# The attention gates of the second block: token columns as stationary operand, 48 weight columns moving

## The chip, the cores and the metric

The kernel runs on one core of one Trainium2 chip. The metric is the device time of one execution in microseconds (us), the median of several. The engines named below are TensorE (PE for its matmuls, PEld for the loads of its stationary operand, which overlap the matmuls), VectorE (DVE), ScalarE (ACT), GpSimd (POOL) and the queue that starts the DMAs (SP).

## The reference

Two transformer blocks over 256 tokens of width 2048, in float32. The change is in the second block, where each of 8 heads has three gates per token (24 columns), which weigh its three attentions:

```
h = modulate(rms_norm_2(x, pre_norm_mix), shift_m, scale_m)      # 256 x 2048
(q_n, k_c, v_c, k_s, v_s, k_w, v_w, g_n, q_m, k_m, v_m) = jnp.split(h @ w_in, split_at, axis=-1)
gates = jax.nn.sigmoid(g_n)                                      # 256 tokens x 24
o_n = g[..., 0:1] * o_c + g[..., 1:2] * o_s + g[..., 2:3] * o_w  # per head
```

So the gate logits are the product of h (256 x 2048) with 24 columns of w_in.

## The kernel before, in words

Every large product is made from values split in two parts, a high one of reduced precision (whi, hH) and the rest (wlo, hL), as three products: high by high, low by high, high by low. A weight unit is a tile of 128 x 1024 (two slices of 128 rows by 512 columns). SP loads it into one of four buffers `raw`; ScalarE writes whi from it (`hi`, L562), VectorE writes wlo (`lo`, L1626), and TensorE makes 12 matmuls of 128x512 from it (`group`, all recorded on L1155, the line of the helper `mm`). Activations are stationary there (128 x 128), weights move.

h of the second block lies transposed in hH and hL: 128 partitions by 16 slices (KT) of 2048 rows, by 256 tokens. The 24 gate columns are loaded once, and split into wgh (ScalarE, L945) and wgl (VectorE, L2116), some 60 us before they are used. The order of the work is written out by hand for each engine. The gates belong to the fourth group of the projections: after unit u of that group TensorE runs a unit of the compression (`cmp_unit`, 16 matmuls with a stationary operand of 60 columns and 128 moving), and after that of unit 0 `gates_mm` (L1497): 48 matmuls, with 24 weight columns stationary and all 256 tokens moving, whose result is 24 x 256. After unit 3 ScalarE applies the sigmoid to it (L982); after unit 5 TensorE turns it back by two transposes (`gates_turn`, L1511), and after unit 7 ScalarE copies the turned 128 x 48 into `gates` (L986), which the attentions read from about 1614 us on. The units of VectorE's loop in this group are L2164 and after, two `lo` for each u.

The engines run ahead of each other only so far as buffers allow: whi and wlo have NSPLIT buffers, and the semaphore w_used tells when TensorE has finished with one.

Of the kernel before, what the change touches and what calls it, by code (L numbers as in the profile page):

```python
# [20 lines left out]
F32 = mybir.dt.float32  # L21
F32R = mybir.dt.float32r
U8 = mybir.dt.uint8
ACT = mybir.ActivationFunctionType
ALU = mybir.AluOpType
AX = mybir.AxisListType
ds = bass.ds

P = 128
T = 256  # L30
TT = T // P
D = 2048
KT = D // P
H = 8
DA = H * P
N_GATE = 24
# [19 lines left out]
BLK = H * T  # L56
# [121 lines left out]
def build(nc, A, out, scratch):  # L178
    with ExitStack() as ctx:
        def sb(name, shape, dt=F32):  # L180
            return ctx.enter_context(nc.sbuf_tensor(name, shape, dt))
# [3 lines left out]
        def S(name):  # L185
            if name not in sems:
                sems[name] = ctx.enter_context(nc.semaphore(name))
            return sems[name]
# [5 lines left out]
        hH = sb("hH", [P, KT, T], F32R)  # L194
        hL = sb("hL", [P, KT, T], F32R)
        yH = sb("yH", [P, H, T], F32R)
        yL = sb("yL", [P, H, T], F32R)
        arena = sb("arena", [P, 11 * BLK + BLK // 2])
# [13 lines left out]
        modA = sb("modA", [P, 4, KT])  # L212
        stat = sb("stat", [P, 4, 3, 2])
        gates = sb("gates", [P, TT, N_GATE])
        wgh = sb("wgh", [P, KT, N_GATE], F32R)
        wgl = sb("wgl", [P, KT, N_GATE], F32R)

        acc = ctx.enter_context(nc.psum_tensor("acc", [P, 2, 2 * GCOL], F32))
        W = ctx.enter_context(nc.psum_tensor("W", [P, 4, 512], F32))
# [8 lines left out]
        def C(name, n=P):  # L228
            return cst[:, CONST[name]:CONST[name] + n]
# [4 lines left out]
        ident, ones = C("ident"), C("ones")  # L234
# [58 lines left out]
        swung = [tokens(b[:, 1024:2048]) for b in turns]  # L293
        wg = blk(7)[:, 0:KT * N_GATE].rearrange("p (k n) -> p k n", k=KT)
        w2 = blk(7)[:, 384:384 + 2 * P].rearrange("p (k n) -> p k n", k=2)
        gateT = arena[0:N_GATE, 11 * BLK + 768:11 * BLK + 768 + T]
        ext = arena[0:H, 10 * BLK:10 * BLK + EXT]
        brow = [blk(0)[:, 1024 + n * GCOL:1024 + (n + 1) * GCOL] if n < 2 else blk(2)[:, n % 2 * GCOL:(n % 2 + 1) * GCOL]
                for n in range(8)]
# [15 lines left out]
        for h in range(H):  # L315
            hd, g = slice(h * T, (h + 1) * T), h // 4
# [236 lines left out]
        def _(act):  # L553
# [68 lines left out]
            for u in range(8):  # L622
                act.wait_ge(S(f"x_in{u}"), 16)
                for j in (2 * u, 2 * u + 1):
                    ins = act.activation(hH[:, j], x0[:, j], ACT.Identity, scale=V("norm_mix", 1, j))
# [316 lines left out]
            root(2)  # L942
            modulated(2, 0, 0, acc[:, (PHASES["cmp_kv"][1] + 1) % 2])
            act.wait_ge(S("wg_in"), 48)
            act.activation(wgh[:], wg[:], ACT.Copy).then_inc(S("wg_hi"), 1)  # L945

            def values(g, v, dst):

# [12 lines left out]
            v2, gg = PHASES["cmp_kv"][0], PHASES["cmp_kv"][1]  # L961
# [16 lines left out]
                act.activation(hsg, hidS, ACT.Sigmoid).then_inc(S("hid_sig"), 1)  # L978

            def gates_sig():  # L980
                act.wait_ge(S("gates_mm"), 1)
                act.activation(gateT, W[0:N_GATE, 2, 0:T], ACT.Sigmoid).then_inc(S("gates_sig"), 1)  # L982

            def gates_copy():
                act.wait_ge(S("gates_turn"), 1)
                act.activation(gates[:].rearrange("p t n -> p (t n)"), W[:, 2, 0:TT * N_GATE], ACT.Copy)\  # L986
                   .then_inc(S("gates_in"), 1)

            def kvc_copy():
                act.wait_ge(S("cmp_kv"), 1)  # L990
# [3 lines left out]
            for u in range(8):  # L994
                hi()
                hi()
                if u == 4:
                    headed(2, gg + 2, qn[:, 1024:2048])()
                if u == 3:
                    gates_sig()  # L1000
                if u == 7:
                    gates_copy()
            pl.g += 1
            group(hooks={3: values(gg + 3, v2 + 39, vsel), 4: hid_sig, 6: headed(3, gg + 3, arena[:, 1024:1536], GCOL),
                         7: kvc_copy})
# [2 lines left out]
            n = N_B  # L1008
# [24 lines left out]
            n = N_N  # L1033
# [117 lines left out]
        def _(pe):  # L1151
            pl = Place()

            def mm(o, l, r, start, stop):
                return pe.matmul(o, l, r, start=start, stop=stop, skip_group_check=True)  # L1155
# [308 lines left out]
            def rope_turn(e, g, heads=GT):  # L1464

                def run():
                    pe.wait_ge(S("roped"), e + 1)
                    for m in range(heads):
                        for t in range(TT):
                            ins = pe.transpose(acc[:, g % 2, m * T + t * P:m * T + (t + 1) * P],  # L1470
                                               roped[e][:, t, m * P:(m + 1) * P], ident)
                    ins.then_inc(S("rope_turn"), 1)
                return run
            gg = PHASES["cmp_kv"][1]
# [22 lines left out]
            def gates_mm():  # L1497

                pe.wait_ge(S("wg_lo"), 1)
                for k in range(KT):  # L1500
                    o = W[0:N_GATE, 2, 0:T]
                    mm(o, wgh[:, k], hH[:, k], k == 0, False)
                    mm(o, wgh[:, k], hL[:, k], False, False)
                    ins = mm(o, wgl[:, k], hH[:, k], False, k == KT - 1)
                ins.then_inc(S("gates_mm"), 1)

            def gates_turn():

                pe.wait_ge(S("gates_sig"), 1)
                for t in range(TT):  # L1510
                    ins = pe.transpose(W[:, 2, t * N_GATE:(t + 1) * N_GATE], gateT[:, t * P:(t + 1) * P],  # L1511
                                       ident[0:N_GATE, 0:N_GATE])
                ins.then_inc(S("gates_turn"), 1)

            def hidden_turn():

# [6 lines left out]
            def compressed():  # L1523
# [3 lines left out]
                for g in range(2):  # L1527
                    ins = mm(W[:, 0, T + g * P:T + (g + 1) * P], hid[:, 1, g], w2[:, 1], True, True)
                ins.then_inc(S("cmp_kv"), 1)
            also_sel = {0: gates_mm, 2: rope_turn(2, gg + 2), 5: gates_turn}  # L1530
            hooks = {u: also(cmp_unit(u // 4, u % 4), also_sel.get(u, lambda: None)) for u in range(8)}
            group(8, hH, hL, (("headed", 2),), hooks=hooks)
            group(8, hH, hL, (("headed", 3),), hooks={1: hidden_turn, 2: rope_turn(3, gg + 3, 2), 5: compressed})
# [2 lines left out]
            n = N_B  # L1536
# [20 lines left out]
            n = N_N  # L1557
# [53 lines left out]
        def _(dve):  # L1611
# [48 lines left out]
            def group(units=8, hooks={}, begin=0):  # L1660
                for u in range(begin, units):
                    lo()
                    if u in hooks:
                        hooks[u]()
                pl.g += 1
# [447 lines left out]
            dve.wait_ge(S("row_cols"), 1)  # L2113
            modulated(2, 2, 0, 0, acc[:, (PHASES["cmp_kv"][1] + 1) % 2])
            dve.wait_ge(S("wg_hi"), 1)
            dve.tensor_tensor(wgl[:], wg, wgh[:].bitcast(F32), ALU.subtract).then_inc(S("wg_lo"), 1)  # L2116

            def rotated(e, g, v, heads=GT):

                def run():
                    dve.wait_ge(S("w_used"), v)
                    if e in (0, 3, 4):
                        dve.wait_ge(S("kv_in"), (0, 3, 4).index(e) + 1)
                    if e:
                        dve.wait_ge(S("rope_turn"), e)
                    h = lambda x: x[:, :, 0:heads * P].rearrange("p t (h d) -> p t h d", d=P)
                    if e == 0:
                        dve.wait_ge(S("rope_in"), 16)
                    tab = lambda name: tokens(rope[name]).unsqueeze(2).to_broadcast([P, TT, heads, P])  # L2130
                    a, r, w = h(tokens(acc[:, g % 2])), h(roped[e]), h(swung[e])
                    d = P // 2
                    dve.tensor_tensor(r, a, tab("cos"), ALU.mult)
                    dve.tensor_tensor(w[..., 0:d], a[..., d:P], tab("sin")[..., 0:d], ALU.mult)
                    then(dve.tensor_tensor(w[..., d:P], a[..., 0:d], tab("sin")[..., d:P], ALU.mult))
                    dve.tensor_tensor(r, r, w, ALU.add).then_inc(S("roped"), 1)
                return run

            def blocks(kind):

                def run():
                    dve.wait_ge(S("headed"), 1)
                    base = arena[:, 0:1]
                    src = bass.AP(base.tensor, base.offset + kind * 2 * T,
                                  [list(base.ap[0]), [1, CMP_LEN], [T, 2], [CMP_STRIDE, N_CMP]])
                    pos = V("v_pos" if kind else "k_pos", CMP_LEN)
                    pos = bass.AP(pos.tensor, pos.offset, [list(pos.ap[0]), [1, CMP_LEN], [0, 2], [0, N_CMP]])
                    o = cx[:, kind * 1024:kind * 1024 + 960].rearrange("p (l g c) -> p l g c", g=2, c=N_CMP)
                    dve.tensor_tensor(o, src, pos, ALU.add).then_inc(S("cx"), 1)
                return run  # L2150

            def blocks_low(kind):
                def run():
                    src = cx[:, kind * 1024:kind * 1024 + 960].rearrange("p (l c) -> p l c", c=30)
                    dve.wait_ge(S("cx_hi"), kind + 1)
                    dve.tensor_tensor(cxp[kind][:, :, 1], src, cxp[kind][:, :, 0].bitcast(F32), ALU.subtract)\
                       .then_inc(S("cx_lo"), 1)
                return run
# [15 lines left out]
            v2, gg = PHASES["cmp_kv"]  # L2174
            group(begin=6)
            pl.phase("qn")
            group(hooks={3: rotated(0, gg, v2 + 8, 2)})
            group(hooks={1: blocks(0), 2: blocks(1), 3: rotated(1, gg + 1, v2 + 16), 6: blocks_low(0), 7: blocks_low(1)})
            for u in range(8):
                lo(2)  # L2180
                if u == 1:
                    rotated(2, gg + 2, v2 + 24)()
            pl.g += 1
            group(hooks={3: also(hidden_rows, rotated(3, gg + 3, v2 + 39, 2)), 5: hidden})
            pl.phase("moba")
            n = N_B
# [15 lines left out]
            n = N_N  # L2202
# [167 lines left out]
```

## Time and profile before

| | |
|---|---|
| median of 3 runs | 2623.61 us (2621.7 to 2624.24) |
| time of the profiled execution | 2621.29 us |
| its span | 2619.5 us |
| mean granted TensorE clock | 0.998 of full |
| PE busy | 2589.9 us (99% of the span) |
| DVE, ACT, POOL busy | 1745.3, 1232.0, 16.5 us |

The span is that of the profiled execution from its first to its last instruction; the time has some 1.8 us around it. PE at 99% does not say that every matmul runs at its peak: a busy TensorE may be waiting inside for its own load of the stationary operand.

### The profile page before, as it was taken

What the parts mean: (1) busy time and instruction counts of PE and PEld (TensorE: products, weight loads), DVE (VectorE), ACT (ScalarE), POOL (GpSimd) and SP (SyncE); (2) the same over time, 40 slices, a digit from 0 to 9 for tenths busy, and PEclk for the clock granted to TensorE, in tenths of its full rate; (3) what the DMA queues carried; (4) which work ended last, traced back from release to release, by engine and by line L of the source; (5) the groups of instructions that cost most, each with busy time, mean ns of one, the idle gap of its engine ahead of it and who ended that gap; (6) DMA issues with size and microseconds to landing.
All of it is one profiled execution on the core that took longest, in us unless ns stands there. A gap on an engine that the chain in (4) does not pass through costs nothing.

```text
span 2619.5 us, 34483 instructions
## 1 busy us (share of the span) xinstructions
PE 2589.9 (99%) x12128; PEld 2158.3 (82%) x12128; DVE 1745.3 (67%) x2106; ACT 1232.0 (47%) x1476; POOL 16.5 (1%) x24
## 2 busy tenths in 40 slices
PE   9999999999999999999999999999999999999998
PEld 7888888888888888888888788888778888888886
DVE  6777668666457777777777777875665555555565
ACT  6444456554454444444444545555544444444343
POOL 0000000000000000000000000000000000000000
PEclk9999999999999999999999999999999999999999
DMA  8876667676558888888877677774466666766664
GB/s 302 279 234 207 214 200 237 200 233 220 191 185 258 256 256 255 251 252 253 253 252 254 182 238 232 218 223 144 139 215 218 210 214 198 230 210 214 210 212 141
DMA packets 281096, 582.27 MB, mean 222 GB/s; under 512 B 17904, under 2 KB 28288, under 8 KB 280336
## 3 DMA queue, kind: packets, MB, share of 16 engines
q1 hardware_dynamic: 279376, 574.25, 69.4%
q0 software_dynamic: 1600, 6.38, 0.8%
q8 instruction: 81, 1.33, 0.2%
q14 instruction: 39, 0.32, 0.0%
HBM read 578.44 MB, written 2.11 MB: 222 GB/s over the span
## 4 chain that ended last, share of the span: by engine, by line
PE 92%; DVE 3%; DMA 2%; ACT 1%; issue 1%; SPq 0%; DVEq 0%; ACTq 0%
PE acc L1155 86%; PE W L1155 4%; DMA raw<-in_w_in 2%; PE W L1204 1%; DVE wlo L1626 1%; DMA raw<-in_w_ada_t 1%; ACT whi L562 1%; PE W L1332 0%; DVE arena L2251 0%; DVE raw L1639 0%; PE acc L1470 0%; PE W L1300 0%; DVE arena L1802 0%; ACT arena L591 0%; ACT arena L634 0%
## 5 line engine op out<-in xcount | busy, mean ns | idle before, releaser
L1626 DVE TENSOR_TENSOR wlo<-raw,whi 128x1024 fp32r<-128x1024 f32 x888 | 1080.6, 1224 | 756.3 <-ACT whi L562 754.2
L562 ACT ACTIVATE whi<-raw 128x1024 fp32r<-128x1024 f32 x888 | 934.1, 1059 | 1123.8 <-PE acc L1155 968.5
L1155 PE MATMUL acc<-whi,hH 128*128 128x512 f32 x2528 | 688.3, 394 | 6.4 <-ACT whi L562 4.0
L1155 PE MATMUL acc<-wlo,hH 128*128 128x512 f32 x2528 | 676.5, 389 | 1.7 <-DVE wlo L1626 1.7
L1155 PE MATMUL acc<-whi,hL 128*128 128x512 f32 x2528 | 676.8, 389 | 0.1
L1155 PEld LDWEIGHTS acc<-wlo,hH 128*128 128x128 f32 x2528 | 474.4, 188 | 102.0 <-DVE wlo L1626 2.6
L1155 PEld LDWEIGHTS acc<-whi,hL 128*128 128x128 f32 x2528 | 474.4, 188 | 101.0 <-DVE hL L1681 1.0
L1155 PEld LDWEIGHTS acc<-whi,hH 128*128 128x128 f32 x2528 | 468.2, 188 | 101.9 <-issue 8.6
L1155 PE MATMUL acc<-whi,yH 128*128 128x512 f32 x992 | 269.5, 393 | 0.0
L1155 PE MATMUL acc<-wlo,yH 128*128 128x512 f32 x992 | 265.4, 389 | 0.0
L1155 PE MATMUL acc<-whi,yL 128*128 128x512 f32 x992 | 265.3, 389 | 0.0
L1639 DVE CUSTOM_DVE_ANT_0 raw<-raw,crow 128x1024 f32<-128x1024 f32 x192 | 234.1, 1219 | 8.6 <-DMA raw<-in_w_ada_t 8.6
L1155 PEld LDWEIGHTS acc<-whi,yL 128*128 128x128 f32 x992 | 186.2, 188 | 39.1
L1155 PEld LDWEIGHTS acc<-wlo,yH 128*128 128x128 f32 x992 | 186.2, 188 | 39.0
L1155 PEld LDWEIGHTS acc<-whi,yH 128*128 128x128 f32 x992 | 185.0, 188 | 37.1
L1155 PE MATMUL W<-arena 128*128 128x128 f32 (+2 forms) x650 | 104.2, 301 | 4.5 <-POOL arena L517 2.6
L1155 PEld LDWEIGHTS W<-arena 128*128 128x128 f32 x650 | 90.2, 194 | 11.8 <-POOL arena L517 2.6
L805 ACT ACTIVATE arena<-arena,stat 128x128 f32<-128x128 f32 x80 | 34.9, 437 | 51.5 <-DVE stat L1948 51.4
L2044 DVE TENSOR_TENSOR arena<-arena,acc 128x1024 f32<-128x1024 f32 x44 | 53.5, 1216 | 0.3 <-PE acc L1155 0.3
L2272 DVE TENSOR_TENSOR yL<-W,yH 128x1024 fp32r<-128x1024 f32 x14 | 17.1, 1224 | 49.6 <-ACT yH L1084 49.6
L1084 ACT ACTIVATE yH<-W 128x1024 fp32r<-128x1024 f32 x14 | 14.4, 1026 | 71.8 <-PE W L1204 71.8
L1204 PE MATMUL W<-cst,arena 128*128 128x128 f32 x312 | 41.0, 275 | 4.8 <-DVE arena L1687 4.8
(192 smaller groups left out, 944.2 us busy)
## 6 DMA issues: line engine op xcount, KB each, us to landing
raw<-in_w_in SPq DMA_DIRECT2D x264, 512.0 KB, 4.7
raw<-in_w_ada_t SPq DMA_DIRECT2D x192, 512.0 KB, 4.8
raw<-in_w_ffn_in SPq DMA_DIRECT2D x176, 512.0 KB, 4.5
raw<-in_w_up SPq DMA_DIRECT2D x128, 512.0 KB, 4.4
raw<-in_w_down SPq DMA_DIRECT2D x128, 512.0 KB, 4.4
raw<-in_w_ffn_out SPq DMA_DIRECT2D x88, 512.0 KB, 4.9
raw<-in_w_out SPq DMA_DIRECT2D x32, 512.0 KB, 4.4
raw<-in_w_o SPq DMA_DIRECT2D x32, 512.0 KB, 3.8
```

The lines of the kernel that those rows point to most:

```text
L562: act.activation(whi[:, v], raw[:, s], ACT.Copy).then_inc(S("w_hi"), 1)
L805: ins = act.activation(p, p, ACT.Exp, bias=stat[:, 1, n % 3, t:t + 1], scale=1.0 if kind == "bias" else SCALE, accum_out=stat[:, 2, n % 3, ...
L1084: act.activation(dst[:, 4 * h:4 * h + 4], tiles(turned), ACT.Copy).then_inc(S("f2_hi"), 1)
L1155: return pe.matmul(o, l, r, start=start, stop=stop, skip_group_check=True)
L1204: ins = pe.transpose(ps[:, m * T + t * P:m * T + (t + 1) * P], src[:, t, m * P:(m + 1) * P], ident)
L1626: dve.tensor_tensor(wlo[:, v], raw[:, s], whi[:, v].bitcast(F32), ALU.subtract)\
L1639: dve.tensor_tensor_reduce(raw[:, s], raw[:, s], crow[:, pl.j % 2 * UW:(pl.j % 2 + 1) * UW], 1.0, 0.0, ALU.mult, ALU.add, o).then_inc(S("u ...
L2044: dve.tensor_tensor(x, x, tokens(acc[:, (PHASES["ffn1"][1] + g) % 2]), ALU.add).then_inc(S("ff_sum"), 1)
L2272: dve.tensor_tensor(lo[:, q], tiles(turned), hi[:, q].bitcast(F32), ALU.subtract).then_inc(S("f2_lo"), 1)
```

## The change

The roles of the operands are exchanged. wgh and wgl become the halves of one tile wgp of 16 x 48 columns. For each of the two token tiles, TensorE loads 128 columns of hH as stationary operand and moves all 48 columns of wgp, then loads the same 128 columns of hL and moves the 24 of wgh. The result has tokens on partitions, in two halves of 24 columns for each token tile (the second half holds high by low). A `tensor_reduce` of VectorE adds the halves into `gates`, and the sigmoid works in place there. The two transposes and the copy are gone.

```
-        wgh = sb("wgh", [P, KT, N_GATE], F32R)
-        wgl = sb("wgl", [P, KT, N_GATE], F32R)
+        wgp = sb("wgp", [P, KT, 2 * N_GATE], F32R)
+        wgh, wgl = wgp[:, :, 0:N_GATE], wgp[:, :, N_GATE:]
...
             def gates_sig():
-                act.wait_ge(S("gates_mm"), 1)
-                act.activation(gateT, W[0:N_GATE, 2, 0:T], ACT.Sigmoid).then_inc(S("gates_sig"), 1)
-
-            def gates_copy():
-                act.wait_ge(S("gates_turn"), 1)
-                act.activation(gates[:].rearrange("p t n -> p (t n)"), W[:, 2, 0:TT * N_GATE], ACT.Copy)\
-                   .then_inc(S("gates_in"), 1)
+                act.wait_ge(S("gates_sum"), 1)
+                g = gates[:].rearrange("p t n -> p (t n)")
+                act.activation(g, g, ACT.Sigmoid).then_inc(S("gates_in"), 1)
...
                 pe.wait_ge(S("wg_lo"), 1)
-                for k in range(KT):
-                    o = W[0:N_GATE, 2, 0:T]
-                    mm(o, wgh[:, k], hH[:, k], k == 0, False)
-                    mm(o, wgh[:, k], hL[:, k], False, False)
-                    ins = mm(o, wgl[:, k], hH[:, k], False, k == KT - 1)
+                for t in range(TT):
+                    o = W[:, 2, t * 2 * N_GATE:(t + 1) * 2 * N_GATE]
+                    for k in range(KT):
+                        c = slice(t * P, (t + 1) * P)
+                        mm(o, hH[:, k, c], wgp[:, k], k == 0, False)
+                        ins = mm(o[:, 0:N_GATE], hL[:, k, c], wgh[:, k], False, k == KT - 1)
                 ins.then_inc(S("gates_mm"), 1)
-
-            def gates_turn():
-
-                pe.wait_ge(S("gates_sig"), 1)
-                for t in range(TT):
-                    ins = pe.transpose(W[:, 2, t * N_GATE:(t + 1) * N_GATE], gateT[:, t * P:(t + 1) * P],
-                                       ident[0:N_GATE, 0:N_GATE])
-                ins.then_inc(S("gates_turn"), 1)
...
-            also_sel = {0: gates_mm, 2: rope_turn(2, gg + 2), 5: gates_turn}
+            also_sel = {0: gates_mm, 2: rope_turn(2, gg + 2)}
...
+            def gates_sum():
+
+                dve.wait_ge(S("gates_mm"), 1)
+                parts_of = W[:, 2, 0:TT * 2 * N_GATE].rearrange("p (t h n) -> p t n h", t=TT, h=2)
+                dve.tensor_reduce(gates[:], parts_of, AX.X, ALU.add).then_inc(S("gates_sum"), 1)
             for u in range(8):
                 lo(2)
                 if u == 1:
                     rotated(2, gg + 2, v2 + 24)()
+                if u == 2:
+                    gates_sum()
```

On TensorE, behind the compression unit of u = 0, the order before has 48 gate matmuls, which go through these three kinds 16 times; further down, behind the compression unit of u = 5, stand the two transposes (the shape is that of the result: 24x256 is a stationary operand of 24 columns with 256 moving):

```order
L1155 MATMUL W<-wlo,yH 60x128
L1155 MATMUL W<-hH,wgh 24x256
L1155 MATMUL W<-hL,wgh 24x256
L1155 MATMUL W<-hH,wgl 24x256
...
L1155 MATMUL acc<-whi,hH 128x512 x4
...
L1511 MATMUL W<-cst,arena 128x24 x2
```

With the change there are 64 at the same place, in 32 pairs of these two kinds (128x48 is a stationary operand of 128 columns with 48 moving), and the row of L1511 is gone:

```order
L1148 MATMUL W<-wlo,yH 60x128
L1148 MATMUL W<-wgp,hH 128x48
L1148 MATMUL W<-wgp,hL 128x24
...
L1148 MATMUL acc<-whi,hH 128x512 x4
L1148 MATMUL acc<-whi,hL 128x512 x4
```

So 48 pairs of a narrow load and a wide matmul become 64 pairs of a wide load and a narrow matmul, in the place where they stood.

On VectorE, in the same group, the order before, from the rope arithmetic of u = 1 (L2133 to L2136) on:

```order
L2133 TENSOR_TENSOR arena<-acc,arena 128x1024 [waits rope_turn,w_used]
L2134 TENSOR_TENSOR arena<-acc,arena 128x8x64
L2135 TENSOR_TENSOR arena<-acc,arena 128x8x64
L2136 TENSOR_TENSOR arena<-arena 128x1024 [waits dve_step]
L1626 TENSOR_TENSOR wlo<-raw,whi 128x1024 [waits w_hi] x16
L2163 COPY arena<-W 60x256 [waits w_used]
```

And with the change, from the last of them on:

```order
L2122 TENSOR_TENSOR arena<-arena 128x1024 [waits dve_step]
L1612 TENSOR_TENSOR wlo<-raw,whi 128x1024 [waits w_hi] x2
L2169 TENSOR_REDUCE gates<-W 128x48 [waits gates_mm]
L1612 TENSOR_TENSOR wlo<-raw,whi 128x1024 [waits w_hi] x14
L2149 COPY arena<-W 60x256 [waits w_used]
```

The new sum stands behind the two low parts of u = 2 and ahead of those of u = 3, and waits for the last gate matmul.

## Rows read from the trace of the kernel before

**Rows 1.** The page, part 1: busy time of each engine.
```profile
PE 2589.9 (99%) x12128; PEld 2158.3 (82%) x12128; DVE 1745.3 (67%) x2106; ACT 1232.0 (47%) x1476; POOL 16.5 (1%) x24
```

**Rows 2.** Chain that ended last, 1515 to 1600 us: start, duration, engine and line.
```profile
1542.08 6.47 PE W L1155 x64
1548.55 2.74 PE acc L1155 x12
...
1563.49 0.97 PE W L1155 x16
```

**Rows 3.** Timeline of PE at the gate matmuls: start, duration, engine, line.
```profile
1542.89 0.27 PE L1155 MATMUL W<-hH,wgh 128*24 128x256 f32 x1
...
1548.27 0.28 PE L1155 MATMUL W<-hH,wgl 128*24 128x256 f32 x1
1548.39 1.09 PE L1155 MATMUL acc<-whi,hH 128*128 128x512 f32 x4
```

**Rows 4.** Loads of the stationary operand, by shape: count, busy us, mean ns.
```profile
L1155 PEld LDWEIGHTS acc<-wlo,hH 128*128 128x128 f32 x2528 | 474.4, 188 | 102.0 <-DVE wlo L1626 2.6
...
L1155 PEld LDWEIGHTS W<-whi,yL 128*60 128x60 f32 x32 | 4.0, 132 | 0.2
...
L1155 PEld LDWEIGHTS W<-hH,wgh 128*24 128x24 f32 x16 | 1.6, 101 | 0.2
```

**Rows 5.** Matmuls by shape: count, busy us, mean ns of one, idle before.
```profile
L1155 PE MATMUL W<-arena 128*128 128x64 f32 x224 | 26.1, 274 | 1.3 <-DVE arena L1845 1.3
```

**Rows 6.** Timeline of PE: three streams with loads of 128 columns.
```profile
268.82 3.68 PE L1155 MATMUL W<-arena 128*128 128x64 f32 x32
...
1461.12 3.29 PE L1155 MATMUL W<-cst 128*128 128x128 f32 x28
...
1581.63 1.07 PE L1155 MATMUL W<-cst,arena 60*128 60x30 f32 x8
```

**Rows 7.** Timeline of PE around the two transposes.
```profile
1564.31 1.14 PE L1155 MATMUL acc<-whi,hH 128*128 128x512 f32 x4
...
1568.16 0.30 PE L1511 MATMUL W<-cst,arena 24*128 24x24 f32 x2
1568.39 1.19 PE L1155 MATMUL acc<-whi,hH 128*128 128x512 f32 x4
...
1572.22 1.14 PE L1155 MATMUL acc<-whi,hH 128*128 128x512 f32 x4
```

**Rows 8.** Timeline of DVE behind the rope arithmetic; one copy from W by itself.
```profile
1545.28 2.35 DVE L1626 TENSOR_TENSOR wlo<-raw,whi 128x1024 fp32r<-128x1024 f32 x2
1552.48 1.22 DVE L1626 TENSOR_TENSOR wlo<-raw,whi 128x1024 fp32r<-128x1024 f32 x1 [4.85 <-ACT whi L562]
...
L2163 DVE COPY arena<-W x1: 409/409/409, 1578.6 to 1578.6; 60x256 f32<-60x256 f32 x1
```

**Rows 9.** Timeline of ACT: table load of the sigmoid, the copy, and what follows.
```profile
1553.43 1.28 ACT L982 ACT_TABLE_LOAD   x1
...
1569.30 0.19 ACT L986 ACTIVATE gates<-W 128x48 f32<-128x48 f32 x1
1571.51 1.06 ACT L562 ACTIVATE whi<-raw 128x1024 fp32r<-128x1024 f32 x1 [2.02 <-PE acc L1155]
```

**Rows 10.** Busy us by engine in four stretches, then clock, DMA share, GB/s.
```profile
268.82:272.30 3.48, 3.48 (x33) 3.47 (x32) 3.26 (x3) 1.06 (x1) 0.00 (x0) 1.00 0.61 179
...
1542.89:1548.39 5.50, 5.50 (x52) 4.86 (x50) 4.71 (x6) 1.32 (x2) 0.00 (x0) 1.00 0.53 137
...
1882.40:1885.90 3.50, 0.01 (x1) 0.00 (x0) 3.10 (x8) 1.88 (x7) 0.00 (x0) 1.00 0.19 36
1885.90:1889.80 3.90, 3.29 (x17) 2.92 (x17) 2.63 (x7) 2.18 (x4) 0.00 (x0) 0.56 0.27 102
```

**Rows 11.** Timeline of PE: eight transposes at the lower clock, eight at the full one.
```profile
1887.30 1.91 PE L1204 MATMUL acc<-cst,arena 128*128 128x128 f32 x8
...
1892.98 1.03 PE L1204 MATMUL W<-cst,arena 128*128 128x128 f32 x8
```

More of the change, by code:

```diff
@@ L295, in build @@
         w2 = blk(7)[:, 384:384 + 2 * P].rearrange("p (k n) -> p k n", k=2)
-        gateT = arena[0:N_GATE, 11 * BLK + 768:11 * BLK + 768 + T]
         ext = arena[0:H, 10 * BLK:10 * BLK + EXT]
@@ L944, in _ @@
             act.wait_ge(S("wg_in"), 48)
-            act.activation(wgh[:], wg[:], ACT.Copy).then_inc(S("wg_hi"), 1)
+            act.activation(wgh, wg[:], ACT.Copy).then_inc(S("wg_hi"), 1)
             def values(g, v, dst):
@@ L1000, in _ @@
                     gates_sig()
-                if u == 7:
-                    gates_copy()
             pl.g += 1
@@ L2115, in _ @@
             dve.wait_ge(S("wg_hi"), 1)
-            dve.tensor_tensor(wgl[:], wg, wgh[:].bitcast(F32), ALU.subtract).then_inc(S("wg_lo"), 1)
+            dve.tensor_tensor(wgl, wg, wgh.bitcast(F32), ALU.subtract).then_inc(S("wg_lo"), 1)
             def rotated(e, g, v, heads=GT):
```

## The prediction

> **What bounds the kernel now.** I read first the page's busy times [rows 1]: PE has 2589.9 of 2619.5 us, so an edit that leaves TensorE's own time alone can hardly move the end. Then the chain of waits through the stretch of the change [rows 2]: from 1542.08 us it is PE on W for 6.47 us (64 matmuls, 16 of the compression and the 48 of the gates) and PE again from 1548.55. No other engine stands between, so the time of the gates is TensorE's and lies on the path. Then the timeline of that stretch [rows 3]: the first gate matmul starts at 1542.89 us, the last at 1548.27, and the next unit at 1548.39. The gates take 1548.39 - 1542.89 = 5.50 us start to start, 5.50 / 48 = 114.6 ns each. The duration in a row (270 to 280 ns) includes the way through the array, which the next matmul overlaps: the cost of a stream of matmuls is the distance of their starts, and I use that alone below.
>
> **What the exchange does to TensorE.** What sets the 114.6 ns? 256 columns move there. In the compression unit 128 move behind a load of 60 columns, and 16 matmuls take 0.97 us in the chain [rows 2], 60.6 ns each. So the two differ by 54 ns for 128 columns, 0.42 ns for a moving column; both streams are bound by the moving side. If that held after the change, 48 and 24 columns would go by very fast. But the stationary side grows from 24 to 128 columns, and there is a floor of its own. The load rows by shape [rows 4] show 101 ns for 24 columns, 132 for 60 and 188 for 128: 31 ns more for 36 columns, 56 for 68, or (188 - 101) / 104 = 0.84 ns a column. 128 columns are then 107 ns of loading, which can hide behind the matmul before only as far as that one lasts. Three streams show the floor directly [rows 6]. Take off the last one's own 0.274 us (the mean of that form [rows 5]; I take the same for all three) from each total and divide by the intervals:
> - 32 matmuls with 64 columns in each record: (3.68 - 0.274) / 31 = 109.9 ns;
> - 28 with 128 columns: (3.29 - 0.275) / 27 = 111.7 ns;
> - 8 with 30 columns: (1.07 - 0.274) / 7 = 113.7 ns.
> A distance that stays at 110 to 114 ns from 30 to 128 columns is not set by the moving side. All three have 128 stationary columns. The two transposes of the gates themselves (24 columns moving, 128 stationary) fit: 1568.16 to 1568.39 is 0.23 us for two [rows 7].
>
 And far below, if loads were hidden fully, the distance of the nearest stream of split parts with a narrow load, 64 x 60.6 = 3.88 us, which is a rival. I take 112 ns, the middle of the streams: 64 x 0.112 = 7.17 us. At the edge to the next unit a little is added: the four matmuls that follow the two transposes show 1.19 us [rows 7] where those behind the gates show 1.09 [rows 3], because a narrow load leaves the next one time and a wide one does not. That is 0.10; I take 0.07 since some of it may be paid at the front. Sum for the gates: 7.24 us against 5.50, **+1.74 us**.
>
> The Trainium skill, in "TensorE: Matmul & The Clock Gate", section "LDWEIGHTS (loading the stationary operand)", states a load as the number of its columns over 1.2 GHz, so 107 ns for 128, and this trace's slope of 0.84 ns a column agrees. The same page's section "Back-to-back issue gap" gives about 81 ns for pairs of a load and a matmul at 128 moving columns; by it an estimate for 64 pairs is 5.2 us, and the change would be a small gain of 0.6 us with the transposes. The streams above, at 110 to 114 ns, speak against it.
>
> **What it removes.** The two transposes are on the path: from unit to unit 1564.31 to 1568.39 is 4.08 us with them, 1568.39 to 1572.22 is 3.83 without [rows 7]. So **-0.25 us**. Between 0.23 (their own starts) and 0.27 there is no more to win, and no wait stands there that would go with them. ScalarE's copy of 0.19 us goes too, but ScalarE stands idle 2.02 us right behind it, waiting for PE [rows 9]: nothing.
>
> **What it adds elsewhere.** The sum of the halves is one reduction of 128x96 to 128x48 on VectorE, with a wait for the last gate matmul. The trace has none of that form; a copy of 256 columns out of W took 0.41 us [rows 8], which I take as the upper end, and zero is the lower. Place and cover: VectorE ends the two low parts of u = 2 at 1547.6 us, and then stood idle 4.85 us to 1552.48, waiting for whi [rows 8]. The gates will end at about 1548.4 + 1.7 = 1550.1, plus some 0.2 for the last to come through; the sum is done at about 1550.7. What is queued behind it is the low part of u = 3, which waits for a whi that waits for PE and so comes at 1552.5 + 1.7 = 1554.2. 3.5 us of cover remain: nothing. If that cover were gone, the price would be at most the 0.4 us. ScalarE's sigmoid now waits for the sum and not for the matmuls; it comes behind its table load, which ends at 1554.7 [rows 9] (some 1.7 us later with the change), so it finds the sum done: nothing. The strided writes of the split weights (24 of each 48 columns) are far ahead of their use, near 1482 us; VectorE and ScalarE each do one there, and I give them zero, with 0.1 us as the upper end. The gates are ready earlier than before and are read only at 1614 us. No DMA is moved or added.
>
> **What is given back later.** Everything behind is shifted by the same amount, as PE is what it waits for. PE waits for others only at a few places behind, where work on the other engines hangs on PE's own results; I take that nothing is given back.
>
> **The sum.** +1.74 - 0.25 = **+1.5 us**. The profiled execution: span 2619.5 + 1.5 = 2621.0 us, time 2621.29 + 1.5 = 2622.8. Its time stands 2.3 us below the median of the runs shown, 2623.61, and 0.4 below their lowest. The forecast for the median is 2623.6 + 1.5 = **2625.1 us**. Own range of the mechanism: 6.85 - 5.50 - 0.27 = +1.1 with nothing at the edge, to 7.28 + 0.10 - 5.50 - 0.23 + 0.5 = +2.2.
>
> **Rivals.**
> 1. *The moving side sets the pace* (chance 9%). Loads of 128 columns are pulled ahead and hidden, and the distance is that of the compression, 60.6 ns, or less. For it: that stream holds its 60.6 ns with a load in each pair. Against: it loads 60 columns, 50 ns by the slope, which fits under the 128 moving; the new pairs load 107 ns and have 10 to 20 ns to move. It gives 3.9 - 5.5 - 0.25 = -1.9 us: 2621.7 us. A partial overlap, at a distance of 80 ns, would give 5.1 - 5.5 - 0.25 = -0.6 us, 2623.0; two of the nine in a hundred are for such.
> 2. *The clock falls* (chance 7%), the one on the slow side. The gates move only 36 columns on average in 112 ns, for 7 us. The granted clock fell once in the body of this run: after PE did nothing from 1882.4 to 1885.9 us, the next 3.9 us had a mean of 0.56, the lower level of 1.2 GHz for most of it [rows 10]. Eight transposes took 1.91 us there and 1.03 after [rows 11]: about twice the distance. For it: the new stretch is longer and thinner than any that the trace has. Against: 32 pairs with 64 columns ran 3.48 us at a clock of 1.00, and so did the gates [rows 10], and the array is never idle in the new stretch. If it falls for half of the gates and as long behind them, that is 3.5 us each at half speed, a loss of 1.7 each: +1.5 + 3.4 = +4.9 us, 2628.5. If it falls for all of the gates the loss is 7 + 1.7, and the time 2633.8. It decides as soon as a granted clock below 1.00 shows between 1543 and 1554 us.
> 3. *The two token tiles in one bank, or the new wait, hold PE* (chance 4%): the next unit's matmul would start late behind the gates. W's part read by VectorE is not used by TensorE until the attentions, and the loops behind wait for whi that are there; with the 0.4 us of the sum on the path it would be +1.9 us: 2625.5.
>
> The forecast has the other 80%. What a measurement of this kernel can tell from no change is about 0.2%, 5.2 us: the forecast of +1.5 us lies inside, and so do rivals 1 and 3, and rival 2 in its milder form. Below 2618.4 there is no case, only a fault of the sum or of the runs: 2%. Above 2628.9 there are the harder half of rival 2 and as much again for the scatter of runs on another chip: 5%. The runs before spread over 2.5 us by themselves, which is more than the forecast moves, so the range takes 2621.5 (rival 1) to 2628.5 (the milder rival 2).
>
> **What would show it.** In the profile of the changed kernel: 64 gate matmuls with distances of 107 to 114 ns whatever they move (48 or 24 columns), loads of 188 ns back to back beside them; 7.1 to 7.4 us from the first to the next unit; no transposes, and a unit of 3.8 us where 4.08 was; a reduction of 0.1 to 0.4 us on VectorE near 1550 us with an idle stretch on both sides; clock 1.00 through it; span near 2621. Distances of 60 ns or less would make the first rival right. A distance that differs between the pairs with 48 and with 24 columns would say that the moving side still counts, and the price of 112 ns would be the wrong term. A change of the span that isn't found in this stretch would say that what I took as a plain shift is not one.

## The result and the profile after

| | before | changed |
|---|---|---|
| median of 20 runs | 2623.51 us (2619.45 to 2626.56) | 2629.62 us (2625.2 to 2633.52) |
| ratio, with 95% interval | | 1.0023 [1.0017, 1.0029] |
| profiled execution: time, span | 2621.29, 2619.5 us | 2628.2, 2626.4 us |
| mean granted clock | 0.998 | 0.995 |

The change costs 6.1 us (4.5 to 7.6 by the interval), where +1.5 was forecast. It lies outside the forecast range by 1.1 us. The busy time of PE against [rows 1]:

```profile
PE 2596.8 (99%) x12142; PEld 2166.1 (82%) x12142; DVE 1745.7 (66%) x2107; ACT 1232.0 (47%) x1475; POOL 16.6 (1%) x24
```

PE is busy 6.9 us longer, as much as the span grew, and its weight loads (PEld) 7.8 us; the other engines are where they were. The timeline of PE in the gate stretch (start, duration, engine, line), to be read against [rows 3]:

```profile
1541.23 0.24 PE L1148 MATMUL W<-wgp,hH 128*128 128x48 f32 x1
...
1545.78 0.26 PE L1148 MATMUL W<-wgp,hL 128*128 128x24 f32 x1
1545.89 0.27 PE L1148 MATMUL W<-wgp,hH 128*128 128x48 f32 x1
1546.00 0.26 PE L1148 MATMUL W<-wgp,hL 128*128 128x24 f32 x1
1546.11 0.33 PE L1148 MATMUL W<-wgp,hH 128*128 128x48 f32 x1
...
1549.89 0.39 PE L1148 MATMUL W<-wgp,hH 128*128 128x48 f32 x1
1550.10 0.37 PE L1148 MATMUL W<-wgp,hL 128*128 128x24 f32 x1
1550.32 2.05 PE L1148 MATMUL acc<-whi,hH 128*128 128x512 f32 x4
...
1555.39 1.14 PE L1148 MATMUL acc<-whi,hH 128*128 128x512 f32 x4
```

Up to 1546.11 us the distances are 110 to 120 ns, the same behind 48 and behind 24 columns. From 1546.26 on they are 210 to 220 ns. The unit behind, whose first four matmuls took 1.09 us in the kernel before [rows 3], begins with 2.05. The same stretches by busy time of each engine (first PE, then PEld, DVE, ACT, POOL, the granted clock, DMA share, GB/s):

```profile
1541.23:1546.11 4.88, 4.88 (x47) 4.88 (x46) 4.71 (x6) 1.32 (x2) 0.00 (x0) 1.00 0.53 154
1546.11:1550.32 4.21, 4.21 (x23) 4.21 (x22) 0.00 (x0) 0.00 (x0) 0.00 (x0) 0.51 0.79 240
1550.32:1555.39 5.07, 5.07 (x29) 4.15 (x30) 0.26 (x1) 0.70 (x1) 0.00 (x0) 0.73 0.00 1
1555.39:1571.33 15.94, 15.94 (x124) 13.71 (x122) 9.45 (x8) 10.56 (x12) 0.00 (x0) 1.00 0.74 209
```

TensorE's clock fell to its lower level of 1.2 GHz 4.9 us into the stretch, and came back in the middle of the unit behind. PE and PEld are both busy for 100% of the stretch in which it fell: the busy share gives no warning here. From the first gate matmul to the second unit behind it are 14.16 us, where the kernel before has 1552.09 - 1542.89 = 9.20.

The two transposes are gone; the unit in whose place they stood, against [rows 7]:

```profile
1567.56 1.14 PE L1148 MATMUL acc<-whi,hH 128*128 128x512 f32 x4
...
1571.33 1.16 PE L1148 MATMUL acc<-whi,hH 128*128 128x512 f32 x4
```

3.77 us where it was 4.08. And the sum on VectorE, against [rows 8]:

```profile
1543.62 2.35 DVE L1612 TENSOR_TENSOR wlo<-raw,whi 128x1024 fp32r<-128x1024 f32 x2
1550.51 0.26 DVE L2169 TENSOR_REDUCE gates<-W 128x48 f32<-128x96 f32 x1 [4.53 <-PE W L1148]
1555.78 2.36 DVE L1612 TENSOR_TENSOR wlo<-raw,whi 128x1024 fp32r<-128x1024 f32 x2 [5.01 <-ACT whi L561]
```

It takes 0.26 us with an idle stretch of 4.5 us ahead and 5.0 behind: hidden, as forecast.

By landmarks of the two profiled executions, the 6.9 us of span come so: -1.7 before the gates (the start differs from execution to execution), +5.0 from the first gate matmul to the second unit behind, -0.4 from there past the place of the transposes (15.94 us where it was 16.30), +2.2 where the clock falls in both kernels near 1886 us, and +1.8 near 2210 us, where PE stood idle for 2.12 us and in the kernel before for 0.35, with no releaser in the profile. So +4.6 of it is the change itself in this execution; the experiments say what it is in others.

### The profile page after: what moved, and what is told of

It is laid out like the page before. It is cut to its first block, busy times and chain, and to the rows that moved or that the text cites. A ratio compares the mean times of both kernels' runs of the same rounds, so it can differ in the third digit from the quotient of the medians.

```text
span 2626.4 us, 34511 instructions
## 1 busy us (share of the span) xinstructions
PE 2596.8 (99%) x12142; PEld 2166.1 (82%) x12142; DVE 1745.7 (66%) x2107; ACT 1232.0 (47%) x1475; POOL 16.6 (1%) x24
## 4 chain that ended last, share of the span: by engine, by line
PE 96%; DVE 1%; ACT 1%; DMA 1%; issue 0%; SPq 0%; DVEq 0%; ACTq 0%
PE acc L1148 89%; PE W L1148 4%; PE W L1197 1%; DMA raw<-in_w_in 1%; PE W L1325 0%; DVE arena L2244 0%; ACT whi L561 0%; DVE wlo L1612 0%; PE acc L1463 0%; PE W L1293 0%; PE acc L1197 0%; ACT arena L590 0%; ACT arena L633 0%; PE W L1208 0%; PE acc L1277 0%
```

## The experiments

Two theories stood against each other. A: the granted clock falls because the 64 pairs move few columns. B: the load floor alone (the 112 ns that a pair takes because of its load of 128 columns; +1.5 us in all), the rest being scatter, or a fall that hangs on the loads, the length or the place. Each difference below is of medians; the ratio with its interval is worked out from the same runs in another way, and the two can differ by a microsecond or so. The comparison is with the runs of the kernel before on the same chip in the same batch (2623.12 us, 33 runs, for the first four; 2622.80 us, 22 runs, for the next four).

**The changed kernel again.**

> The changed kernel once more, timed beside the kernel before and the three edits below. Theory A (the granted clock falls in the gate stretch because its pairs move few columns): +5 to +7 us over the kernel before, and a stretch at half clock that begins some 3 to 6 us after the first gate matmul. Theory B (the load floor alone, +1.5 us; the rest of the +6.1 us is scatter of the other, later fall of the clock): +1 to +3 us this time, and the clock full between the first gate matmul and the next unit in some profiles.

2629.05 us (11 runs), +5.9 us, ratio 1.0019 [1.001, 1.0028]. The first gate matmul started at 1544.48 us and the second unit behind at 1558.61: 14.13 us, with the unit between them again at 2.05 us for its first four. The slowdown repeats.

**The same loads, 128 columns moved.**

```
-                        c = slice(t * P, (t + 1) * P)
-                        mm(o, hH[:, k, c], wgp[:, k], k == 0, False)
-                        ins = mm(o[:, 0:N_GATE], hL[:, k, c], wgh[:, k], False, k == KT - 1)
+                        c, m = slice(t * P, (t + 1) * P), wgq[:, k * 2 * N_GATE:k * 2 * N_GATE + P]
+                        mm(o, hH[:, k, c], m, k == 0, False)
+                        ins = mm(o, hL[:, k, c], m, False, k == KT - 1)
```

(P is 128. wgq is wgp with 128 more columns at its end, so that the last slice can move 128 too; only the gates' own columns of the result are read.)

> The changed kernel with 128 columns moved in each of the 64 gate matmuls (the first 48 are the gates' columns, the others are not read; the stationary loads are the same 64 of 128 columns). Theory A: the clock stays at 1.00 through the stretch, the distance stays 110 to 112 ns, the stretch is 7.1 to 7.3 us, and the time is +1.5 us over the kernel before (0 to +3 with the scatter), 4 to 5 us under the changed kernel. Theory B, or a fall that hangs on the loads or on the length of the stretch and not on the columns: the same time as the changed kernel within 1.5 us, with the half clock still there.

2624.64 us (11 runs), +1.5 us, ratio 1.0005 [0.9996, 1.0014]; 4.4 us faster than the changed kernel beside it. In its timeline the unit behind the gates has its normal length, 3.76 us:

```profile
1550.78 1.14 PE L1150 MATMUL acc<-whi,hH 128*128 128x512 f32 x4
...
1554.54 1.16 PE L1150 MATMUL acc<-whi,hH 128*128 128x512 f32 x4
```

The busy times of the gate stretch by engine, with the clock (columns as above):

```profile
1543.60:1550.80 7.20, 7.20 (x69) 7.20 (x66) 4.74 (x6) 1.35 (x2) 0.00 (x0) 1.00 0.63 186
```

The groups of its gate matmuls (line, engine, count, minimum, median and maximum duration in ns, first and last start):

```profile
L1150 PE MATMUL W<-wgq,hH x32: 273/276/278, 1543.6 to 1550.6; 128*128 128x128 f32 x32
L1150 PE MATMUL W<-wgq,hL x32: 272/274/276, 1543.7 to 1550.7; 128*128 128x128 f32 x32
```

64 matmuls in 7.2 us, 112 ns each, at full clock: 128 columns moved in place of 48 and 24 cost nothing by themselves, because the load sets the pace, and with them the clock stays. This is theory A's number. It also agrees with the forecast's +1.5 us, as well as an interval from -1.0 to +3.7 us can say: the forecast priced everything but the clock. Columns moved, columns read and columns written go together in these matmuls, so the runs don't tell which of them matters.

**The same pairs in four parts.** The sum and the sigmoid come later, behind the last part.

```
-            also_sel = {0: gates_mm, 2: rope_turn(2, gg + 2)}
+            also_sel = {0: gates_part(0), 1: gates_part(1), 2: also(gates_part(2), rope_turn(2, gg + 2)), 3: gates_part(3)}
```

> The changed kernel with its 64 gate matmuls in four parts of 16, one behind each of the units 0 to 3 (sum and sigmoid moved behind the last part); the work is the same. Theory A: each thin stretch is only 1.8 us between dense units, the clock stays at 1.00, the time is +1.5 to +2 us over the kernel before (four edges in place of one). Theory B: as the changed kernel, within 1.5 us. If the half clock comes though the columns are spread, then the thin pairs cost the clock in whatever portion.

2624.82 us (11 runs), +1.7 us, ratio 1.0006 [0.9997, 1.0015]. The first part, and the stretch with the other three (columns as above):

```profile
1547.70:1549.50 1.80, 1.80 (x21) 1.80 (x19) 1.77 (x4) 1.36 (x2) 0.00 (x0) 1.00 0.72 203
1549.50:1569.00 19.50, 19.50 (x151) 17.43 (x150) 10.24 (x10) 7.10 (x7) 0.00 (x0) 1.00 0.65 182
```

The same thin pairs brought no fall in portions of 1.8 us between dense units. So it isn't the pair itself but a longer run of them.

**Two parts.** As before, with 32 matmuls behind units 0 and 3 each.

```
+            also_sel = {0: gates_part(0), 2: rope_turn(2, gg + 2), 3: gates_part(1)}
```

> The changed kernel with its gate matmuls in two parts of 32, behind units 0 and 3 (sum and sigmoid later, as in the version in four parts). Each thin stretch is 3.6 us. Theory A gives no number for how long is too long: if no fall, +1.5 us over the kernel before as with four parts; if a fall in some runs or in one of the parts, +2 to +5 us and a wider scatter than with four parts. Theory B: as the changed kernel, +6 us.

2627.95 us (11 runs, 2625.1 to 2633.64), +5.2 us, ratio 1.0025 [1.0016, 1.0034]: about as slow as the changed kernel, and its runs lie wider apart than those with four parts (8.5 us against 4.3). Here each part and the unit behind it:

```profile
1545.50:1549.02 3.52, 3.52 (x36) 3.52 (x33) 3.48 (x5) 1.29 (x2) 0.00 (x0) 1.00 0.57 162
1549.02:1554.42 5.40, 5.40 (x31) 4.41 (x30) 1.20 (x2) 0.70 (x1) 0.00 (x0) 0.68 0.68 195
1562.80:1566.54 3.74, 3.74 (x36) 3.74 (x34) 2.36 (x2) 1.34 (x2) 0.00 (x0) 0.95 0.83 219
1566.54:1571.75 5.21, 5.21 (x29) 4.28 (x30) 0.26 (x1) 0.69 (x1) 0.00 (x0) 0.71 0.54 170
```

The clock fell twice, once for each part, and the price was mostly paid in the dense unit behind (5.40 and 5.21 us where that unit takes 3.70). That is 3.2 us; with the load floor's 1.7, less 0.3 for the transposes, it makes 4.6 of the 5.2 us.

**Thin and wide pairs at another place.** The kernel before, unchanged, with 64 more matmuls in the group before, between dense units.

```
+                        mm(o[:, 0:48], hH[:, k, c], m[:, 0:48], k == 0, False)
+                        mm(o[:, 0:24], hL[:, k, c], m[:, 0:24], False, k == KT - 1)
...
+                        mm(o, hH[:, k, c], m[:, 0:P], k == 0, False)
+                        mm(o, hL[:, k, c], m[:, 0:P], False, k == KT - 1)
```

(The first two lines are the thin pair of one kernel, the last two the wide pair of the other.)

> The kernel before, unchanged, plus 64 extra matmuls with the loads and columns of the new gates (128 stationary, 48 and 24 moving; their result is overwritten) in the group before, behind its unit 5, with dense units on both sides. Theory A: the load floor makes 64 x 0.112 = 7.2 us, and a fall of the clock begins in or just behind the extra stretch and costs about 3.4 more: +10 to +11.5 us over the kernel before. Theory B (the fall in the changed kernel needed the narrow compression matmuls beside it, or the place): +6.5 to +8 us with the clock at 1.00.

> The same 64 extra matmuls at the same place with 128 columns moved in each: same loads. Both theories: +6.5 to +8 us over the kernel before, the clock at 1.00, the distance 110 to 112 ns. The difference to the thin version is the price of the fall alone: 3 to 4 us by theory A, nothing by theory B.

Thin: 2636.95 us (5 runs), +14.2 us, ratio 1.0058 [1.0044, 1.0071]. Wide: 2629.22 us (6 runs), +6.4 us, ratio 1.0031 [1.0018, 1.0043]. The thin stretch in two pieces and the unit behind, then the wide stretch of the other kernel:

```profile
1533.20:1536.50 3.30, 3.30 (x32) 3.29 (x30) 2.26 (x3) 2.12 (x2) 0.00 (x0) 1.00 1.06 327
1536.50:1543.59 7.09, 7.09 (x37) 7.09 (x36) 0.75 (x1) 0.00 (x0) 0.00 (x0) 0.51 0.56 163
1543.59:1547.95 4.36, 4.36 (x13) 3.47 (x14) 0.00 (x0) 0.00 (x0) 0.00 (x0) 0.62 0.00 0
```

```profile
1533.80:1540.87 7.07, 7.07 (x65) 7.07 (x64) 3.36 (x3) 2.12 (x2) 0.00 (x0) 1.00 0.99 295
```

The wide stretch costs its load floor, 7.07 us in the profile, and nothing more (+6.4 us in the medians, just under the 6.5 to 8 expected). The thin one brings the fall with it, far from the compression unit, so the place is not the cause. Its price was larger than the 3.4 us expected, and its +14.2 us lies above the 10 to 11.5 expected: in the profile 14.75 us to the second unit behind against 1543.69 - 1533.80 = 9.89, so 4.9; in the medians 7.7, of five and six runs. What the other 2.8 us are is open.

**How long the fall lasts.** Two more profiles of the changed kernel and one of the kernel before.

> The changed kernel, one more profile. Theory A: the clock falls again inside the gate stretch, 3 to 6 us after the first gate matmul, and is back 6.8 us later or so; from the first gate matmul to the second unit behind (9.20 us before) it takes 13.5 to 15.5 us. If it lasts longer in this execution than in the two seen (14.2 us), the rest of the measured +6 us over the local +4.6 is explained by its length; if all look alike, that rest is scatter of the fall near 1886 us.

> The same once more: 13.5 to 15.5 us from the first gate matmul to the second unit behind, clock at half for about half of that.

> The kernel before, one more profile: 9.2 us from the first gate matmul to the second unit behind, clock 1.00 there; near 1886 us (the transposes behind the idle of 3.5 us) the half clock comes in any case, and the 10.7 us that its four groups of eight transposes spanned may differ by 1 to 2 us from execution to execution, as the changed kernel's 11.0 and 12.9 did.

The changed kernel, first of the two (2629.24 us): first gate matmul, second piece, and the unit behind.

```profile
1542.42:1546.20 3.78, 3.78 (x37) 3.78 (x35) 3.75 (x6) 1.32 (x2) 0.00 (x0) 0.98 0.53 155
1546.20:1552.70 6.50, 6.50 (x33) 6.50 (x32) 0.97 (x1) 0.00 (x0) 0.00 (x0) 0.50 0.56 161
1552.70:1557.90 5.20, 5.20 (x25) 4.19 (x26) 0.26 (x1) 0.42 (x1) 0.00 (x0) 0.65 0.00 0
```

The second (2633.94 us):

```profile
1546.97:1550.50 3.53, 3.53 (x33) 3.53 (x32) 3.50 (x6) 1.32 (x2) 0.00 (x0) 0.94 0.60 186
1550.50:1557.77 7.27, 7.27 (x35) 7.27 (x36) 1.22 (x2) 0.00 (x0) 0.00 (x0) 0.50 0.50 145
1557.77:1563.50 5.73, 5.73 (x18) 4.46 (x19) 0.26 (x1) 0.17 (x1) 0.00 (x0) 0.50 0.00 0
```

In all four profiles of this kernel the clock falls in the gate stretch, but at another moment: from the first gate matmul to the second unit behind it took 14.16, 14.13, 15.76 and 17.33 us. My bound of 15.5 was too low for two of them. The mean, 15.35, is 6.15 us over the 9.20 of before; less the 0.3 to 0.4 of the transposes it is +5.8 us. That is about the measured +6.1 and +5.9, though the four lie 3.2 us apart, so that so close an agreement is in part luck. The kernel before, in its second profile (2626.64 us), had its unit behind the gates at normal length (start, duration):

```profile
1552.13 1.09 PE L1155 MATMUL acc<-whi,hH 128*128 128x512 f32 x4
...
1555.83 1.16 PE L1155 MATMUL acc<-whi,hH 128*128 128x512 f32 x4
```

3.70 us, as in the first. The stretch near 1886 us took 10.2 us there, from the first of its transposes (1890.83) to the last group's (1900.98), against 10.7 in the first, and 12.9, 11.0, 13.1 and 10.7 in the four of the changed kernel. The fall there comes in both kernels. Whether it also lasts longer behind the thin stretch is open: in the seven profiles without a fall at the gates or at the added pairs it took 10.2 to 11.1 us, in the six with a fall there 10.7 to 13.1, with a mean of 11.9.

**A form that is better than both.** High and low weight columns stacked to 48 stationary columns, with all 256 tokens moving; the edit is shown against the kernel before.

```
-                    mm(o, wgh[:, k], hH[:, k], k == 0, False)
-                    mm(o, wgh[:, k], hL[:, k], False, False)
-                    ins = mm(o, wgl[:, k], hH[:, k], False, k == KT - 1)
+                    mm(W[0:2 * N_GATE, 2, 0:T], wgp[:, k], hH[:, k], k == 0, False)
+                    ins = mm(W[0:N_GATE, 2, 0:T], wgh[:, k], hL[:, k], False, k == KT - 1)
```

(The copy out of W, the two transposes, VectorE's sum of the halves and the sigmoid follow.)

> A third form of the gates: high and low weight columns stacked to 48 stationary columns, all 256 tokens moving; 16 matmuls of 48 columns with hH and 16 of 24 columns with hL, then two transposes of 48 rows, the sum on VectorE and the sigmoid. Both theories expect the moving side to bound (256 columns at 114.6 ns, a load of 48 columns is 40 ns): 32 x 0.1146 = 3.67 us where the kernel before has 5.50, so -1.8 us against the kernel before, with the clock at 1.00; in the whole time -0.5 to -3 us. It would be the best version of the four.

> The stacked form (48 stationary columns, 256 moving) again, on whatever chip this batch gets: -1.8 us against the kernel before by its matmuls (-1 to -3.5 us measured). A time equal to the kernel before would say that the first batch's -3.3 us was scatter.

First batch: 2619.85 us (11 runs), -3.3 us, ratio 0.9989 [0.998, 0.9998]. Second: 2620.93 us (11 runs), -1.9 us, ratio 0.9997 [0.9988, 1.0006]. Its stretch in the first batch's profile, and the loads and matmuls with hH (columns as above):

```profile
1545.10:1548.80 3.70, 3.70 (x36) 3.46 (x33) 3.67 (x5) 1.30 (x2) 0.00 (x0) 1.00 0.56 157
```

```profile
L1153 PEld LDWEIGHTS W<-hH,wgp x16: 120/121/123, 1545.0 to 1548.4; 128*48 128x48 f32 x16
L1153 PE MATMUL W<-hH,wgp x16: 276/278/281, 1545.1 to 1548.6; 128*48 128x256 f32 x16
```

32 matmuls in 3.7 us, 116 ns each, in place of 48 in 5.50: -1.8 us in the trace. The wider load costs nothing behind 256 moving columns. Both medians have the sign, the second ratio is worth only -0.8 us, and only one of the two intervals excludes no change; the gain is shown in the stretch, and in the whole time it is likely.

## Why the prediction was wrong

- *The load floor*: right. Forecast 112 ns a pair and 7.24 us for the gates; the version with 128 columns has 7.2 us at full clock, and the first 44 distances of the changed kernel have a mean of 110.9 ns. The distance didn't hang on the columns. The first rival (the moving side sets the pace) is out. With it goes the figure of about 81 ns for a pair in the Trainium skill, "TensorE: Matmul & The Clock Gate", section "Back-to-back issue gap": pairs with 128 columns moving took 112 ns here.
- *The transposes*: -0.25 forecast, -0.31 found between the units' starts.
- *The sum, the sigmoid, the strided writes*: nothing, as forecast; the sum took 0.26 us inside 9.8 us of cover.
- *The shift*: right; between 1571.33 and 1888.86 us the changed kernel took as long as the one before between 1568.39 and 1885.93 (317.5 us both).
- *The clock*: this is the step that failed. The sum took all 64 matmuls at 112 ns, the distance at the full clock, and put a fall of the clock at nothing, for the gates and for the unit behind. The runs showed a fall in its place: it is worth 4.4 us between the changed kernel and the version with 128 columns moved. It was rival 2, priced fairly (+4.9 us for its milder form, +10 for the harder; in the profiles it was +4.6 to +7.8), but with a chance of 7%. That the milder form, with the fall for just half of the gates, comes within 1.1 us of the measured median is in part luck, as the moment of the fall differs so much. It came in every one of four profiles. The reason I put against it, that "the array is never idle in the new stretch", took a busy engine for one whose clock is safe: PE was busy for 100% of the stretch, and the clock fell. The other, that 32 pairs with 64 columns ran 3.48 us at full clock [rows 10], was a stretch of half the length and of unsplit float32, too far from the case to carry 93%. The thin stretch was longer than anything the trace had, and I had said so: a resource that the trace doesn't show should have kept both ends in the range, which would have reached past 2630.

The Trainium skill, in "TensorE: Matmul & The Clock Gate", section "HAM oscillation — how this bites in real kernels", gives as an abstract rule that there be no long idle gaps of TensorE. Here it was kept and was not enough: with no gap at all and PE and PEld busy for 100%, the clock fell to 1.2 GHz. The Trainium skill's section "LDWEIGHTS (loading the stationary operand)" on the same page gives the load as its columns over 1.2 GHz. That agrees at the full clock (an estimate of 107 ns by it, against the 112 of a pair), and not at the lower one, where a pair took 213 ns on average (1546.48 to 1550.10 us, 17 distances).

## What to carry to other kernels

Before the operands of a small product are exchanged, compare the two floors: what moves, and what is loaded. Here a pair bound by 128 loaded columns took as long as one bound by 256 moved ones (112 and 115 ns), so the exchange traded 48 matmuls for 64 at nearly the same price each. And a run of matmuls that are bound by their loads moves few columns, and can cost TensorE's clock for itself and for the dense work behind it, though every busy share says 100%: break it into short parts between dense work, let it move more columns for nothing, or better, load fewer columns and move more.

## What the runs showed of the hardware that was not expected

- The clock fell in a stretch in which PE and PEld were busy without a gap, moving 36 columns in each 112 ns on average. Moving 128 in the same time, with the same loads, it stayed at full.
- In the profile with four parts of 1.8 us between dense units the clock stayed at 1.00; in the one with two parts of 3.5 us it was 0.68 and 0.71 in the unit behind each.
- The load of the stationary operand slows with the clock: pairs bound by it went from 111 to 213 ns, and the durations of the loads themselves from 192 to 333 ns (median and maximum in the changed kernel):

```profile
L1148 PEld LDWEIGHTS W<-wgp,hH x32: 189/192/333, 1541.2 to 1549.8; 128*128 128x128 f32 x32
```

- When in the stretch the clock falls, and so the price, differs between executions of one kernel: 5.0, 5.7, 3.7 and 3.1 us behind the first gate matmul in the four profiles, and 14.16, 14.13, 15.76 and 17.33 us for the same work.
